# Experts in unsplit float32 on four column strips of the array, 96 tokens a job, a ring of 14 weight tiles

## The reference, cut to what matters

```python
def moe_ffn(h, w_router, w_gate, w_up, w_down):
    logits = (h @ w_router).astype(jnp.float32)
    top_logit, top_idx = lax.top_k(logits, TOP_E)            # TOP_E = 2 of N_EXP = 8
    gates = jax.nn.softmax(top_logit, axis=-1)
    ...
    for e in range(N_EXP):
        out = out + combine[..., e:e + 1] * swiglu(h, w_gate[e], w_up[e], w_down[e])
```

## Time and profile before

| | us |
|---|---|
| median of 3 runs | 1398.5 (1398.44 to 1398.61) |
| span of the profiled execution, first to last instruction | 1396.7 |
| TensorE busy in it | 1386.0 (99%) |
| VectorE busy | 1141.3 (82%) |
| ScalarE busy | 987.6 (71%) |
| GpSimd busy | 80.7 (6%) |
| bytes moved | 440.16 MB, mean 315 GB/s |
| first product of the jobs starts at | 439.2 |
| first product of the last scatter starts at | 1386.5 |

### The profile page before, as it was taken

The page is one execution under the profiler, slowest core; times in us unless marked ns, Lnnn a source line. Parts: engine busy times, 40 slices in busy tenths (PEclk is TensorE's granted clock), DMA queues, the critical chain, the costliest instruction groups (busy, mean ns, idle before and its releaser), DMA issues.

```text
span 1396.7 us, 18564 instructions
## 1 busy us (share of the span) xinstructions
PE 1386.0 (99%) x6628; PEld 1149.5 (82%) x6628; DVE 1141.3 (82%) x1110; ACT 987.6 (71%) x968; POOL 80.7 (6%) x105
## 2 busy tenths in 40 slices
PE   9999999999999999999999999999999999999997
PEld 8878888888878888888888888888888888888886
DVE  6786555566787988888888898888889889888997
ACT  7676543346677777877877877787787778778776
POOL 2012000002116200000000000000000000001100
PEclk9999999999999999999999999999999999999999
DMA  9427755555335999999999999999999999999994
GB/s 340 161 92 265 268 197 189 181 181 178 125 104 211 382 387 386 389 388 387 389 388 387 376 389 387 384 372 388 387 367 388 387 363 384 388 366 381 390 387 151
DMA packets 218544, 440.16 MB, mean 315 GB/s; under 512 B 7407, under 2 KB 11681, under 8 KB 218497
## 3 DMA queue, kind: packets, MB, share of 16 engines
q1 hardware_dynamic: 214000, 424.61, 84.0%
q0 software_dynamic: 3472, 11.27, 2.2%
q10 hardware_dynamic: 1024, 3.67, 0.6%
HBM read 426.93 MB, written 12.59 MB: 315 GB/s over the span
## 4 chain that ended last, share of the span: by engine, by line
PE 97%; DVE 1%; DMA 0%; ACT 0%; issue 0%; DVEq 0%; SPq 0%
PE bank L1801 30%; PE bank L1796 30%; PE bank L1797 29%; PE bank L2438 2%; PE bank L1992 1%; PE bank L2073 1%; PE bank L2064 0%; PE bank L2398 0%; PE bank L2263 0%; PE bank L2049 0%; PE bank L1837 0%; DMA x_sb<-in_x_dram 0%; PE bank L2180 0%; PE bank L2057 0%; PE bank L1790 0%; PE bank L1792 0%
## 5 line engine op out<-in xcount | busy, mean ns | idle before, releaser
L1100 DVE TENSOR_TENSOR w_lo<-raw,w_hi 128x2048 fp32r<-128x2048 f32 x335 | 758.0, 2289 | 86.8 <-ACT w_hi L507 86.3
L507 ACT ACTIVATE w_hi<-raw 128x2048 fp32r<-128x2048 f32 x336 | 642.9, 1919 | 145.8 <-PE bank L1801 143.5
L1796 PE MATMUL bank<-w_hi,xg_hi 128*128 128x512 f32 x896 | 351.0, 392 | 0.0
L1797 PE MATMUL bank<-w_hi,xg_lo 128*128 128x512 f32 x896 | 348.8, 389 | 0.0
L1801 PE MATMUL bank<-w_lo,xg_hi 128*128 128x512 f32 x896 | 240.1, 390 | 0.1
L1796 PE MATMUL bank<-w_hi,ht_hi 128*128 128x512 f32 x528 | 206.3, 391 | 0.0
L1797 PE MATMUL bank<-w_hi,ht_lo 128*128 128x512 f32 x528 | 205.6, 389 | 0.0
L1801 PEld LDWEIGHTS bank<-w_lo,xg_hi 128*128 128x128 f32 x896 | 167.9, 188 | 36.5 <-DVE w_lo L1100 1.4
L1797 PEld LDWEIGHTS bank<-w_hi,xg_lo 128*128 128x128 f32 x896 | 168.3, 188 | 34.2
L1796 PEld LDWEIGHTS bank<-w_hi,xg_hi 128*128 128x128 f32 x896 | 168.3, 188 | 34.1
L1070 DVE TENSOR_TENSOR w_lo<-raw,w_hi 128x2048 fp32r<-128x2048 f32 (+4 forms) x52 | 114.5, 2211 | 43.7 <-ACT w_hi L477 42.8
(11 more groups left out here) (341 smaller groups left out, 1055.1 us busy)
## 6 DMA issues: line engine op xcount, KB each, us to landing
raw<-in_od_w_gate_e_dram SPq DMA_DIRECT2D x112, 1024.0 KB, 9.0
raw<-in_od_w_up_e_dram SPq DMA_DIRECT2D x112, 1024.0 KB, 9.2
raw<-in_od_w_down_e_dram SPq DMA_DIRECT2D x112, 1024.0 KB, 9.6
raw<-in_od_w_qkv_dram SPq DMA_DIRECT2D x12, 1024.0 KB, 5.2
raw<-in_ev_w_gate_dram SPq DMA_DIRECT2D x11, 1024.0 KB, 5.2
raw<-in_ev_w_up_dram SPq DMA_DIRECT2D x11, 1024.0 KB, 5.0
raw<-in_ev_w_down_dram SPq DMA_DIRECT2D x11, 1024.0 KB, 5.0
raw<-in_ev_w_in_dram SPq DMA_DIRECT2D x6, 1024.0 KB, 15.1
```

What stands on the lines that cost most here:

```text
L507: act.activation(w_hi[:, g % HL, :], raw[:, g % RAW, :], ACT.Copy).then_inc(hi_ready, 1)
L1100: dve.tensor_tensor(w_lo[:, g % HL, :], raw[:, g % RAW, :], w_hi[:, g % HL, :].bitcast(F32), ALU.subtract)\
L1796: pe.matmul(out_ap, l_hi, r_hi, start=first, stop=False)
L1797: pe.matmul(out_ap, l_lo, r_hi, start=False, stop=False)
```

## The change

The jobs change, and what surrounds them in so far as it touches them.

- A job takes up to 96 tokens (`CAP`) instead of 128, and there may be five further jobs instead of three (`MAX_OVER`).
- Weights and tokens of the jobs are used as float32, straight from the landed tile. `job_hi`, `job_lo`, the lo parts of `xg` and `ht` and their semaphores are gone. The room of `raw`, `w_hi`, `w_lo` and `xt_lo` becomes one ring of 14 tiles (`RING`). SP may load a tile once TensorE has used the one 14 before (`tile_used`); in the first job the slots 7 to 12 wait for the last use of the split tiles and slot 13 for the router's product.
- The width 3584 is cut into slices of 1024, 1024, 1024 and 512 (`WIDTHS`), with the loads in the order of `ORDER`. A tile of a wide slice or of down is two chunks of 1024 columns (4 KB rows), a tile of the last slice four chunks of 512.
- A product is made on four column strips of the array (`strips`). Strips 0 to 2 hold 32 tokens each and take quarter q of the columns; strip 3 takes the fourth quarter for the tokens of group q. Three rounds q = 0, 1, 2 over all tiles of the product complete it. A round's call has 256 moving columns (128 in the last slice). Tiles are given back in the third round.
- The result of strip 3 has another layout: `turn_h` transposes six pieces a wide slice and three in the last (banks 7 and 3), `h_slice` finds the tokens in it, and VectorE copies the fourth quarter of y out by itself (`tail_out`).
- The places of further jobs are computed for 96 slots, also twice for one expert.

The core of the diff:

```diff
-AHEAD = 3
-E_STEPS = D_FF_E // 512
-JOB = 6 * E_STEPS
-MAX_OVER = 3
+RING = 14
+WIDTHS = [1024, 1024, 1024, 512]
+E_STEPS = len(WIDTHS)
+ORDER = [("gate", 0), ("up", 0), ("gate", 1), ("up", 1), ("down", 0), ("gate", 2), ("up", 2), ("down", 1),
+         ("gate", 3), ("up", 3), ("down", 2), ("down", 3)]
+JOB = 42
+CAP = 96
+MAX_OVER = 5
...
@@ SP
-                            s = (T_MOE + i) % RAW
-                            sp.wait_ge(lo_ready, j * JOB + T_MOE + i - RAW + 1)
-                            sp.dma_start(slot(raw, s, 4, 512), src).then_inc(raw_landed[s], 16)
+                        slot_i = ring_slot(i)
+                        if not first or i >= RING:
+                            sp.wait_ge(tile_used, j * JOB + T_MOE + i - RING + 1)
+                        elif i < RAW:
+                            sp.wait_ge(lo_ready, T_MOE + i - RAW + 1)
+                        elif i < RAW + 2 * HL:
+                            sp.wait_ge(tile_used, T_MOE)
+                        else:
+                            sp.wait_ge(logits, 1)
+                        sp.dma_start(ring[:, slot_i].rearrange("p (c f) -> p c f", f=src.shape[-1]), src)\
+                            .then_inc(ring_landed[slot_i], 16)
...
@@ ScalarE
+            def gate_out(j, s):
+                act.wait_ge(tile_used, j * JOB + T_MOE + TILES["gate", s][-1] + 1)
+                if s:
+                    act.wait_ge(m_h, j * E_STEPS + s)
+                n = 3 * WIDTHS[s] // 4
+                one = act.activation(m_sg[:, 0:min(n, 512)], B[0][:, 0:min(n, 512)], ACT.Silu)
+                if n > 512:
+                    one = act.activation(m_sg[:, 512:n], B[1][:, 0:n - 512], ACT.Silu)
+                one.then_inc(m_silu, 1)
+            def turned_out(j, s):
+                act.wait_ge(m_t, j * E_STEPS + s + 1)
+                ...  m_ht <- banks 7 and 3 ... .then_inc(m_turned, 1)
...
@@ VectorE
+                for s in range(E_STEPS):
+                    dve.wait_ge(tile_used, j * JOB + T_MOE + TILES["up", s][-1] + 1)
+                    dve.wait_ge(m_silu, j * E_STEPS + s + 1)
+                    if s:
+                        dve.wait_ge(m_t, j * E_STEPS + s)
+                    ...  m_hh <- m_sg * banks 2 and 3 ... .then_inc(m_h, 1)
...
@@ TensorE
+            def strips(q_bank, n, q, tokens, w, first, last):
+                bank, c0 = q_bank
+                for g in range(3):
+                    pe.matmul(B[bank][32 * g:32 * g + 32, c0:c0 + n], tokens(g), w[:, n * q:n * q + n],
+                              start=first, stop=last, tile_position=(0, 32 * g))
+                return pe.matmul(B[bank][96:P, c0:c0 + n], tokens(q), w[:, 3 * n:4 * n],
+                                 start=first, stop=last, tile_position=(0, 96))
...
+            def wide(j, kind, s):
+                chunks, n = TW // WIDTHS[s], WIDTHS[s] // 4
+                for q in range(3):
+                    if q == 2 and kind == "up" and s in (1, 2):
+                        pe.wait_ge(m_turned, j * E_STEPS + s)
+                    for k, i in enumerate(TILES[kind, s]):
+                        if q == 0:
+                            ...
+                            landed(j, i)
+                        for c in range(chunks):
+                            kc = chunks * k + c
+                            m = strips(place(kind, s, q), n, q, lambda g: xg[:, kc, 32 * g:32 * g + 32], weights(i, chunks)[:, c],
+                                       kc == 0, kc == KC - 1)
+                        if q == 2:
+                            m.then_inc(tile_used, 1)
...
+                for s in range(E_STEPS):
+                    if s:
+                        pe.wait_ge(m_silu, j * E_STEPS + s)
+                    wide(j, "gate", s)
+                    if s:
+                        turn_h(j, s - 1)
+                    if s == 3 and last:
+                        turn_sel()
+                    wide(j, "up", s)
+                    if s in (1, 2):
+                        if s == 1:
+                            pe.wait_ge(y_out, j * 3 + 3)
+                            pe.wait_ge(y_tail_out, j * 3 + 3)
+                        down(j, s - 1)
+                pe.wait_ge(m_turned, j * E_STEPS + 3)
+                down(j, 2, [0])
+                turn_h(j, 3)
+                if not last:
+                    turn_next(j)
+                down(j, 2, [1, 2])
+                pe.wait_ge(m_turned, j * E_STEPS + 4)
+                down(j, 3, last=last)
```

More of the change, by code:

```diff
@@ L70 @@
 QKV_COLS = [0, 1024, 2048, 512, 1536, 2560]
[L71 to L72 removed]
+NEXT_X = 28
 COEF, RECIP_1, HEAD_MS, LAM, NEG_LAM, LAST_MS = 16, 32, 64, 80, 84, 88
@@ L93, in ffn_tiles, with job_tiles, ring_slot, place @@
     return [], [], [32]
[L96 to L107, removed]
+def job_tiles():
+    tiles, i = {}, 0
+    for kind, s in ORDER:
+        n = 4 if WIDTHS[s] == 1024 else 2
+        tiles[kind, s] = list(range(i, i + n))
+        i += n
+    assert i == JOB and JOB % RING == 0
+    return tiles
+TILES = job_tiles()
+def ring_slot(i):
+    return (T_MOE + i) % RAW if i % RING < RAW else i % RING
+def place(kind, s, q):
+    w = WIDTHS[s] // 4
+    if kind == "down":
+        return 4 + q, 0
+    bank = 0 if kind == "gate" else 2
+    return (bank + q // 2, q % 2 * w) if w == 256 else (bank, q * w)
 def trunk(nc, a):
@@ L225, in trunk @@
         raw_landed = [sem(f"raw_landed{i}") for i in range(RAW)]
+        ring_landed = raw_landed + [sem(f"ring_landed{i}") for i in range(RAW, RING)]
         hi_ready = sem("hi_ready")
@@ L407, in _, with load @@
                     sp.dma_start(dst, src).then_inc(raw_landed[i % RAW], 16)
-            def load(j, e, wanted, last=False):
+            def load(j, e, first=False, last=False):
                 gate_w = a["od_w_gate_e"][0, bass.ds(e, 1)].rearrange("o (c p) f -> p (o c) f", p=P)
@@ L437, in _ @@
+            load(0, 0, first=True)
+            with sp.Fori(1, LAST) as j:
+                load(j, j)
             sp.wait_ge(routed, 1)
@@ L1751, in _, with leave @@
+            def leave(j):
+                dve.wait_ge(y_stored, j * 16 + 16)
+                dve.wait_ge(tile_used, j * JOB + T_MOE + JOB)
+                for q in range(3):
+                    tail_out(q).then_inc(y_tail_out, 1)
+            dve.engine_nop().then_inc(y_out, 3)
+            dve.engine_nop().then_inc(y_tail_out, 3)
             dve.engine_nop().then_inc(y_stored, 16)
@@ L1753, in _ @@
                 job(j)
-                for i in range(AHEAD):
-                    job_lo(j + 1, i)
+                leave(j)
             job(n_over + LAST, last=True)
-            add_rows(1, 1)
             dve.wait_ge(late_landed, 32)
@@ new lines, in strips, with landed @@
+            def strips(q_bank, n, q, tokens, w, first, last):
[5 more added lines that the diff above has]
+                                 start=first, stop=last, tile_position=(0, 96))
+            def landed(j, i):
+                before = sum(t % RAW == ring_slot(i) for t in range(T_MOE))
+                pe.wait_ge(ring_landed[ring_slot(i)], j * (16 * JOB // RING) + 16 * (before + i // RING + 1))
@@ new lines, in h_slice, with down @@
+            def h_slice(s, c, g):
+                full = 3 * WIDTHS[s] // 512
+                at = (c * P + 32 * g) if c < full else ((full // 3 * g + c - full) * P + 96)
+                return m_ht[:, s % 2, at:at + 32]
+            def down(j, s, quarters=range(3), last=False):
+                for q in quarters:
+                    for k, i in enumerate(TILES["down", s]):
+                        if q == 0:
+                            landed(j, i)
+                        for c in range(2):
+                            m = strips(place("down", s, q), 256, q, lambda g: h_slice(s, 2 * k + c, g), weights(i, 2)[:, c],
+                                       s == 0 and k == 0 and c == 0, s == E_STEPS - 1 and k == 1 and c == 1)
+                        if q == 2:
+                            m.then_inc(tile_used, 1)
+                    if last and q < 2:
+                        m.then_inc(y_part_done, 1)
```

353 lines of the change are left out of this document (121 added, 232 removed).

## The result

The changed kernel takes 1484.9 us (1477.9 to 1486.7), the kernel before on the same chip 1398.5 us: a ratio of 1.061 [1.059, 1.063]. The forecast was 1370 us with a range of 1343 to 1412; the kernel is slower, and outside the range. The profiled execution has a span of 1484.6 us.

The account below looks back on a forecast made before the run. TensorE was taken to bound the kernel, transfers close behind. Eight jobs of 113.9 us, less 0.7, plus 8.4 for jumps gave 918.9 against 947.2 us, so 28.3 off the median of 1398.5: 1370 us, range 1343 to 1412.

Parts of the forecast that it names:

- What bounds it, and the product: Expert stage: TensorE sets the time; four strips run at once at 0.216 us a step, products 109.2 us a job.
- the sum: Expert stage: 113.9 us a job for eight jobs, with jumps and ends 918.9 us against 947.2.
- jump term: TensorE's jump back at the loop's end: refetching instructions costs 1.2 us, seven times, 8.4 us.
- (2): Product on column strips: four separate streams exceed a read limit, a step takes twice as long, 2244 us; chance 0.11.
- (3): TensorE in the jobs: it can't take records this fast, 132.5 us a job, 1519 us; chance 0.03.
- Changes between strips and the whole array: Around the transposes in a job: 0.3 us for each of four sandwiches, 1.5 us a job with the first record after each.
- VectorE, ScalarE, transfers: Expert stage: removed split work gains nothing, remaining copies are covered by products, and loads keep up at 396 GB/s.
- booking nothing: Weight loads in the expert stage: no time added for transfers, since a ring of 14 tiles covers 26 us.
- the estimate: Loads with 4 KB rows: 7% more data per unit of queue share, 4 to 12% with rounding.
- rival (1): Loop's end: the jump costs 5 to 9.0 us, its fetch behind 1 MiB transfers, 1397 to 1425 us; chance 0.11.

Follow-up runs that it names:

- narrow part merged, and written out: The changed kernel with the last slice's gate and up products in 6 calls a chunk instead of 12, and TensorE's jobs written out instead of looped: 1363.3 us.
- narrow part merged: The changed kernel with the last slice's gate and up products in 6 calls a chunk instead of 12, TensorE's jobs still looped: 1428.3 us.
- light loads: The changed kernel with loads of experts' weights from the second job on bringing only a sixteenth of each row, same instructions: 1400.4 us.
- the written out kernel: The changed kernel with TensorE's jobs written out one after the other instead of looped: 1408.8 us.

## Why the prediction was wrong

**What bounds it, and the product.** Right. Four column strips run at once at 0.216 us a step (0.21 + 0.01 in the chain above) and 0.11 for 128 columns, so the rivals (2) and (3) are out: four pairs of records in 0.11 us are 0.03 us a pair. A job whose instructions come in time takes 113.2 us; the sum had 113.9. The sum without its jump term is 1361.6 us, and the kernel with jumps and narrow stalls repaired runs 1363.3. In part that is luck: eight jobs 0.7 us shorter than summed are 5.6 us, so what lies outside of the steady jobs took some 7 us more than it had in the sum. The Trainium skill, "TensorE: Matmul & The Clock Gate", Part 3, says that packed tiles side by side gain; here the trace agrees, at 0.216 us for four.

**Changes between strips and the whole array.** Right in the main, 0.3 us for each. The weight load stands before each group of transposes:

```profile
PEld bank L2459 <- issue: 11.5, 32, 0.4
```

That is 0.36 us for each of 32 in the changed kernel, part of it under running matmuls. By the starts of the matmuls, a group of six takes 0.26 us more than its 0.11 us a piece, and the group of eleven 0.16: 0.9 us a job where 1.5 was summed.

**VectorE, ScalarE, transfers.** Right in the changed kernel: no wait of TensorE for any of them, and a landing of 10.9 us (9.0 before). But that kernel is slow enough to leave the loads time. Where the instructions come in time (narrow part merged, and written out), landing takes 18.2 us of the 26 that the ring covers, and TensorE waits 3.2 us in all for transfers; booking nothing was nearly right, with little reserve. Of that kernel, a line of the page and one of the waits:

```profile
ring<-in_od_w_gate_e_dram SPq DMA_DIRECT2D x112, 1024.0 KB, 18.2
...
PE bank L2401 <- DMA ring<-in_od_w_up_e_dram: 2.4, 1, 2.4
```

The 4 KB rows bring 397 GB/s over a job of the merged kernel at a share of 1.03, where 383 at 1.04 came before, 5% more for a unit of share, within the 4 to 12% of the estimate.

**The jump: mis-sized, by a factor of nine.** The step took the landing of a 64 KB block in an early, quiet stretch as the nearest row, 1.2 us, and put the landing of a tile under load at the upper end. The price is 10.8 us (narrow part merged) to 12.7 (not merged), above that end too. Three parts were missed. The fetch is slow because of the loads, which light loads show (a first standing of 5.0 to 5.6 us becomes 2.2 to 2.6); rival (1) had this, and its counter-argument, that 16 KB are a 64th of a tile, was false, since the time isn't in the bytes: each block is on its way for 1 us. One fetch doesn't end it: the block with the target lasted 21 matmuls and their weight loads, and a second wait followed. And the granted clock falls to 1.2 GHz with the standing, for some 10 us a jump, which the profile charges to "busy": TensorE's busy time is 1387.6 us in the changed kernel and 1342.3 in the merged and written out one. Half of the busy time that lies in stretches at the lower clock is 33.7 us; the rest of that difference I can't place. There are six jumps, not seven. Instead of 8.4 us this is 65.0 us (narrow part merged), and that kernel's rows give it: 48.8 us of standing and 16.7 lost at the lower clock, 65.5.

**The rate of instructions in straight code: a term that was missing.** I counted the 4,474 instructions only for whether they fit, and the records' rate only against TensorE's own pace. Neither asks how fast they can be brought. The prediction's own numbers gave the demand, 4,474 instructions are 17.5 blocks in 109 us and twice that rate in the narrow part. What rows of before couldn't give is the supply: with 27 blocks in all, the queue was never short. The narrow part cost 56.6 us. With 65.0 for the jumps and 1.7 for the rest of the sum, that is the 123.3 us from 1361.6 to 1484.9. The split depends on the order of the repairs: written out first, it is 76.1 us for the jumps back and 45.5 for the narrow part and the jump forward.

The Trainium skill, "Runtime: NRT & Kernel Launch", section Instruction fetch mechanics, has the refetch after a taken jump whose target isn't in a window of two pages. q8 bears out the refetch, with 173 blocks where the written out kernel has 160. It doesn't bear out the size of the window: the loop body of the kernel before, some 1,080 records and so more than four blocks, stayed held, and one of two such jobs didn't (58 blocks). Of a crossing from block to block it says that the cost is "mostly hidden". Here the measurement decides: hidden at 6.9 us a block and more, not at 3.5.

## What to carry to other kernels

When a change multiplies an engine's instructions, divide the instructions of the densest stretch, not of the whole job, into blocks and set the time of one against what the instruction queue can bring beside the kernel's loads (here a block every 6.2 us); and price a loop's jump, once its body isn't held, as two waits and the slow clock behind them. Fewer, wider calls (here 384 and 512 columns in three groups beside narrow ones in the fourth) stream the same columns and repair the first; writing the jobs out repairs the second. In a profile, "issue" idle that recurs at the same place of every job, each ending 1.3 to 1.8 us after a block on q8, is the sign. And a part that a slow kernel leaves without a wait, as the loads here, has to be looked at again once the kernel is repaired.

## What the hardware did that I had not expected

- TensorE's instructions, 16 KB a block: in straight code a block 6.2 us after the last while TensorE is starved beside some 400 GB/s of loads, 3.3 to 4.2 us in the narrow part beside 32 GB/s, and 0.9 to 1.4 us from start to end of the transfer in most cases in both. What the rest of the 6.2 us is, the records don't show, and I didn't test it further. It isn't a least distance of two transfers: at the six jumps of the changed kernel the target's block starts 3.0 to 3.9 us after the block before it, beside 400 GB/s.
- TensorE goes on 1.3 to 1.8 us after a block's end.
- With 5 us of standing the granted clock falls to 0.5, in the changed kernel for 3.4 to 13.7 us at a time; after the three narrow stalls of 1.3 to 2.5 us it does so for 3.4 us in seven jobs of the changed kernel, and in three jobs of the written out one.
- A call of 512 columns in three column groups and two of 256 in the fourth run side by side without loss.
